# Storing the routed rows from two queues, and the order of four other steps between a router and its expert loop

## The reference

```
v_in = rms_norm(h, norm_ffn_w)                       # 512 rows of 1024
g_logits = vf @ w_rg + b_rg                          # 4 groups; the best one is kept
e_sel = e_logits of that group                       # 8 experts; the best two are kept
gate = softmax(top_v) * p_g                          # two gates for each token
# tokens are sorted by expert into padded blocks, one block at least per expert here
hu = v_pad[tok_b] @ w_e_in[e]                        # 1024 -> 2 x 512
y  = (silu(a) * u) @ w_e_out[e] * gate               # 512 -> 1024, added into the token's row
```

## Time and profile before

| | us |
|---|---|
| median of three executions | 2727.82 (2725.10 to 2729.26) |
| the profiled execution | 2725.17 |
| its span in the profile | 2723.9 |
| `Route` and what leads to the first expert product | 706 to 743 |
| the expert loop | 743 to about 1205 |

### The profile page before, as it was taken

One profiled execution on the slowest core, in us unless ns is written; L12 is line 12 of the kernel. 1 busy time (PEld: TensorE's weight loads), 2 busy tenths in 40 slices (PEclk: granted clock), 3 DMA queues, 4 the chain that ended last, 5 costly groups with the idle time before them and its releaser, 6 DMA issues.

```text
span 2723.9 us, 38632 instructions
## 1 busy us (share of the span) xinstructions
PE 2627.2 (96%) x16282; PEld 2065.9 (76%) x16282; DVE 1286.9 (47%) x2277; ACT 898.7 (33%) x1328; POOL 148.7 (5%) x201
## 2 busy tenths in 40 slices
PE   8999999999999989999999999999999999999997
PEld 6778888778744333349999999988879786788885
DVE  4445666534423333356344465544544434644444
ACT  4334555333221111123222243444444322432222
POOL 0000000000100000000000000031230400000000
PEclk9999999999899999999999999999999999999998
DMA  3012212144599999963222222211111222322221
GB/s 144 16 64 66 61 58 62 58 140 139 218 414 420 421 420 421 420 285 117 94 86 94 81 76 83 96 59 51 59 59 44 66 93 87 103 99 93 93 90 57
DMA packets 78203, 381.62 MB, mean 140 GB/s; under 512 B 9944, under 2 KB 10200, under 8 KB 52816
## 3 DMA queue, kind: packets, MB, share of 16 engines
q1 hardware_dynamic: 71856, 357.14, 35.7%
q0 software_dynamic: 5456, 20.11, 1.9%
q10 hardware_dynamic: 720, 1.90, 0.2%
HBM read 372.67 MB, written 10.62 MB: 141 GB/s over the span
## 4 chain that ended last, share of the span: by engine, by line
PE 74%; DMA 8%; DVE 4%; SPq 2%; ACT 2%; issue 1%; DVEq 0%; ACTq 0%
PE ps L208 72%; DMA rmore<-in_w_ein 5%; DMA ring<-in_w_ein 2%; SPq L293 2%; PE ps L212 1%; DVE ringr L581 0%; PE ps L1963 0%; DMA ring<-in_w_hg 0%; ACT L218 0%; ACT ringr L575 0%; DVE hT L2666 0%; DVE uT L472 0%; ACT hdd L1230 0%; DVE hT L3958 0%; DVE mgb L3955 0%
## 5 line engine op out<-in xcount | busy, mean ns | idle before, releaser
L208 PE MATMUL ps<-uh,ringr 128*128 128x264 f32 (+1 forms) x2256 | 553.8, 340 | 4.4 <-DVE uTr L619 2.4
L208 PEld LDWEIGHTS ps<-uh,ringr 128*128 128x128 f32 x2256 | 366.6, 189 | 48.7 <-DVE uTr L619 3.6
L208 PE MATMUL ps<-buh,ringr 128*128 128x512 f32 (+1 forms) x1312 | 347.2, 351 | 4.4 <-ACT hg L1212 3.3
L208 PE MATMUL ps<-uTr,ringr 128*128 128x512 f32 (+1 forms) x1136 | 350.5, 345 | 0.0
L581 DVE TENSOR_TENSOR ringr<-ring,ringr 128x1024 fp32r<-128x1024 f32 (+1 forms) x215 | 258.2, 1212 | 141.2 <-ACT ringr L575 140.6
L575 ACT CAST ringr<-ring 128x1024 fp32r<-128x1024 f32 (+1 forms) x215 | 219.4, 1036 | 92.8 <-DMA ring<-in_w_fi 34.3
L208 PEld LDWEIGHTS ps<-buh,ringr 128*128 128x128 f32 x1312 | 218.9, 189 | 35.5 <-issue 7.4
L208 PEld LDWEIGHTS ps<-uTr,ringr 128*128 128x128 f32 x1136 | 197.4, 189 | 22.5 <-issue 3.1
L208 PE MATMUL ps<-ful,ringr 128*128 128x264 f32 (+1 forms) x648 | 169.9, 323 | 0.2 <-DVE ful L508 0.2
L208 PE MATMUL ps<-fhh,ringr 128*128 128x264 f32 (+1 forms) x576 | 123.7, 321 | 0.0
L2627 DVE TENSOR_TENSOR fsg<-ps,fsg 128x528 f32<-128x528 f32 (+1 forms) x44 | 30.8, 700 | 193.5 <-PE ps L208 189.7
(11 more groups left out here) (485 smaller groups left out, 4553.5 us busy)
## 6 DMA issues: line engine op xcount, KB each, us to landing
rmore<-in_w_ein SPq DMA_DIRECT2D x51, 1024.0 KB, 27.0
eahead<-in_w_ein SPq DMA_DIRECT2D x47, 1024.0 KB, 26.7
ring<-in_w_ein SPq DMA_DIRECT2D x30, 1024.0 KB, 27.0
rmore<-in_w_eout SPq DMA_DIRECT2D x27, 1024.0 KB, 27.0
ring<-in_w_fi SPq DMA_DIRECT2D x54, 512.0 KB, 3.7
ring<-in_w_eout SPq DMA_DIRECT2D x19, 1024.0 KB, 27.3
eahead<-in_w_eout SPq DMA_DIRECT2D x18, 1024.0 KB, 27.3
fmore<-in_w_fi SPq DMA_DIRECT2D x34, 512.0 KB, 3.7
```

What stands on the lines that cost most here:

```text
L208: return self.P.matmul(out, lhsT, rhs, start=start, stop=stop, skip_group_check=True)
```

## The change

Five edits, all in `Route` but the last:

- The stores of rows 1 and 3 are issued by ScalarE, right after it has written the block, from its own DMA queue, instead of by GpSimd. GpSimd keeps rows 0 and 2.
- ScalarE makes the fourth block of rows before the second exponential (`vexp`) instead of behind it. The store of row 3 goes with it.
- VectorE works out the count of blocks between the two groups of pick products, instead of behind the second group, the overflow lists, the gates and a square of the meta tokens (`meta_dve`).
- The semaphores of the two stores come from the set for hardware queues.
- The idle products ahead of expert 0 go from 11 to 6.

```diff
-        self.rows = [sig.pdma(f"rows{i}") for i in range(4)]
+        self.rows = [(sig.dma if i % 2 else sig.pdma)(f"rows{i}") for i in range(4)]
@@ row_act
             A.activation(self.sent[:, i, 512 * j:512 * j + 512], ps[:, b + j, :], ACT.Copy, scale=self.rt[:, i:i + 1]).then_inc(
                 self.rowed.next(), 1)
+        if i % 2:
+            A.wait_ge(*self.rowed.at(2 * i + 2))
+            A.dma_start(self.k.vrow[128 * i:128 * i + 128, :], self.sent[:, i, :]).then_inc(self.rows[i].landing(), 16)
@@ act
         self.row_act(1)
         self.row_act(2)
+        self.row_act(3)
         v2 = self.s[:, 5, 0:4]
         A.wait_ge(*self.vdiff.at(1))
         A.activation(v2, v2, ACT.Exp).then_inc(self.vexp.next(), 1)
-        self.row_act(3)
@@ pool
-        for i in range(4):
+        for i in (0, 2):
             G.wait_ge(*self.rowed.at(2 * i + 2))
@@ place_dve
         V.tensor_scalar(self.pair, k.ps[:, b, 0:NE // 2], -1.0, float(S), MUL, ADD).then_inc(self.given.next(), 1)
-        V.wait_ge(*self.pick.at(2))
-        over = k.ps[0:64, b + 1, NBLK:NBLK + NOV]
-        V.tensor_scalar(self.more, over, -1.0, float(S), MUL, ADD).then_inc(self.given.next(), 1)
-        V.tensor_scalar(self.tokens, over, -1.0, float(S), MUL, ADD).then_inc(self.given.next(), 1)
-        V.tensor_copy(self.gates, k.ps[:, b + 1, 0:NBLK]).then_inc(self.given.next(), 1)
-        self.nxt.meta_dve()
         V.tensor_tensor(self.cmp, end[0:1].unsqueeze(1).to_broadcast([1, NOV, 32]),
                         iota[0:1, 0:NOV].unsqueeze(2).to_broadcast([1, NOV, 32]), ALU.is_le).then_inc(s.next(), 1)
         V.wait_ge(*s.last())
...
         V.tensor_copy(self.ov[:, 0:1], end[0:1, 31:32]).then_inc(self.blocks.next(), 1)
+        V.wait_ge(*self.pick.at(2))
+        over = k.ps[0:64, b + 1, NBLK:NBLK + NOV]
+        V.tensor_scalar(self.more, over, -1.0, float(S), MUL, ADD).then_inc(self.given.next(), 1)
+        V.tensor_scalar(self.tokens, over, -1.0, float(S), MUL, ADD).then_inc(self.given.next(), 1)
+        V.tensor_copy(self.gates, k.ps[:, b + 1, 0:NBLK]).then_inc(self.given.next(), 1)
+        self.nxt.meta_dve()
@@ Experts.pe
-        self.k.busy(6, 11)
+        self.k.busy(6, 6)
```

## The result

The changed kernel takes 2729.36 us (median of 20 executions, 2725.00 to 2732.88). The kernel before, on the same chips, takes 2725.92 (20 executions, 2723.71 to 2729.26). The ratio is 1.0013, 95% interval 1.0008 to 1.0019: **3.4 us slower**. That is inside the stated range and inside the 0.2% that was called no change. But it is clear of noise and of the other sign than the forecast of -0.6 us.

The account below looks back on a forecast made before the run. The loop's end was taken to be set by when the weight stream resumes behind the hole, after expert 0's first slot. Earlier gather -1.2 us plus clock +0.6 gave -0.6 us: 2727.2 us against a median of 2727.82, range 2722.7 to 2731.

Parts of the forecast that it names:

- The hole as the only path: Weight stream ahead of expert loop: the first expert product moves the hole's end and, one for one, the kernel's end.
- Stores: Row stores ahead of the gather: with a second queue, 105 GB/s each, the last lands at about 729.6 instead of 734.4.
- `vexp`: ScalarE's second exponential, behind the fourth block: comes at 720.0 to 720.4 instead of 719.71, a delay taken as 0.4 us.
- GpSimd ... clears `xg` earlier; nobody waited for that: GpSimd loses two store issues of 0.53 us and clears the gather's buffer earlier; no cost was counted.
- The list at 730.75: Index list `idx` that the gather needs: 730.34 before, plus 0.4 us from the delay of `vexp`.
- The gather's 8.4 us: First gather, issued at 731.85, takes 8.4 us and lands at 740.2 against 740.97; first product 1.2 us earlier, at 741.65.
- Case 2: First gather keeps its 5.5 us: product at 738.8, -2.3 to -4.1 us, 2724.6 us; chance 0.15.
- The clock, +0.6 us: Expert 0 starts at the half level in most executions; 1.8 us for one slow slot, 2.8 for two, 0.6 taken on average.
- How the clock got there: TensorE ahead of expert 0: 12 idle products at the half level, 2.7 us, then a pause of about 3 us.
- Case 3: First two slots of expert 0: half clock costs more than the gather gives, +1.6 to +2.8 us, 2729.4 us; chance 0.17.
- Cases 4 and 5: Row 3's store served late, past 734.4, +4.9 us, chance 0.08; second queue brings nothing, 0 within 0.5 us, chance 0.10.
- "Same" at 0.92: Whole kernel: chance 0.92 of no change beyond about 0.2%, 5.5 us; faster 0.05, slower 0.03.

Follow-up runs that it names:

- the early clearing: Kernel before the change, with GpSimd's clearing of `xg` moved ahead of its store of row 3; ratio 1.0002 (0.9993 to 1.0011).
- the decisive run: Changed kernel with 24 idle products ahead of expert 0 instead of 6, nothing else; ratio 1.0000 (0.9992 to 1.0009) to the kernel before.
- the clearing later: Changed kernel with GpSimd clearing `xg` only when VectorE has the sum of both choices; ratio 1.0007 (0.9999 to 1.0016) to the kernel before.
- all five loads held: Changed kernel with SP's last five loads ahead of the loop waiting for the first gather's landing; ratio 1.0013 (1.0004 to 1.0022) to the kernel before.
- three loads and 6 idle products: Changed kernel, clearing late, 6 idle products, SP's last three loads held until the second pick group ends; ratio 0.9990 (0.9981 to 0.9999) to the kernel before.

## Why the prediction was wrong, step by step

- **The hole as the only path: right in the main.** The stream's lag of 1.20 MB stays constant through the loop, and over the kernels with the full backlog the ratio roughly follows the hole's end. But the prediction gave as a sign of being wrong that the loop's end moves by something that the hole doesn't, and it moved by 4.8 us against 2.7; that part is open.
- **Stores: right in direction and nearly in size.** The last one was expected at 729.6; it was issued at 719.61, took 11.2 us and landed at 730.8, ahead of the list. The rule of the Trainium skill weighed there (page "DMA: Bandwidth & Descriptors", section "Issuing engines are not separate DMA queues"), that issuing from several engines saves only issue time, was not borne out: four stores were there 17.2 us after the first one's issue instead of 20.8. Row 3 was issued 1.75 us earlier here, but with the two stores alone, where it was issued as late as before, they were there after 17.3 us too. The estimate behind 729.6, 105 GB/s for each queue, was not measured by itself.
- **`vexp`: right.** Expected at 720.0 to 720.4, found at 720.01. ScalarE's queue was held for 0.35 us.
- **"GpSimd ... clears `xg` earlier; nobody waited for that": the first step that failed, a term put at nothing.** Nobody waits for its result, but VectorE waits for the clearing itself: 0.69 us on the chain. I had looked at who reads the outcome of a moved instruction, not at what it runs beside.
- **The list at 730.75: missed, 732.54.** 0.3 us are `vexp`, 0.7 the clearing. The rest, 1.2 us, is in idle products: TensorE waited 1.14 us for VectorE, the clock fell within 724 to 725, and the 24 idle products behind took 7.23 us instead of 5.6 and were now what the pick products waited for. I had costed the delay of the chain at its own length and overlooked that a fixed number of idle products takes longer at the half level. This 1.2 us doesn't belong to the change alone: with the fewer idle products or the early clearing, edits that touch nothing of this chain, the list stood at 17.8 too, behind pauses of 1.84 us, since in those executions the idle products behind the rows' transposes began 1.7 us earlier.
- **The gather's 8.4 us: right, and with it that most of the earlier issue is lost.** It took 8.4. A fixed time behind the issue is not what the runs show, though: with the full backlog the gather landed 26.5 to 28.3 us after row 0's store whether it was issued at 18.3 or at 22.0, and issued at 19.9 and 20.0 it landed at 28.3 and 27.5. So what the late list costs by the landing isn't fixed by these single executions. The upper end of the prediction, 741.4, "since the bytes of the stretch are the same", lies nearest: 741.9. Case 2, a quick gather, is out: 7.5 to 8.9 us in every kernel that issued it by 20.0 with the backlog there.
- **The clock, +0.6 us: the term of the sum that failed in size, and the one that the decisive run is about.** The text said that expert 0 would start at the half level "in most executions", priced that at 1.8 us for one slot, and then took 0.6. The profile shows 1.74 us for the first slot and 0.4 for the transposes, which ran at the half level too, 2.1 us in all. With the price of one slot in full, the sum would have been -1.2 + 1.8 = +0.6, slower. The run with 24 idle products gives the 3.4 us back with the list as late as in the changed kernel, while the earlier list alone (the clearing later) gave nothing that is clear of noise.
- **How the clock got there: partly wrong.** The prediction had it low since 730 to 732 and not yet up again. Here it was up: the idle products ran at the full level, the pause was 5.58 us instead of about 3 (half a microsecond from their earlier end, 1.7 from the later landing), and the clock fell at the end of the pause. The pause was seen, but the half level was laid to too short a run of idle products. With all five loads held the run was as short, 12 instructions, the pause 0.59 us, and expert 0 took 7.09 us.
- **The two misses together.** The first product came at 743.82, not at 741.65: 1.8 us for the late list, if it is taken in full, and 0.4 for the slow transposes. So the profile's account is +0.97 + 1.74 = +2.7, beside 3.4 between the medians. Either miss by itself would have turned the sign: -0.6 + 1.8 = +1.2 for the list, +0.6 for the clock.
- **Case 3 is what happened in its mechanism,** given 0.17 and +1.6 to +2.8 us; measured +3.4. Its sum is made of other parts, though: it had the first product 1.2 us earlier and two slow slots at 2.8, and the profile has the product 0.97 later and 1.74 until the first slot is free. Cases 4 and 5 are out: row 3 landed at 730.8.
- **"Same" at 0.92 was right by the bound of 0.2%**, and 2729.36 lies in the range, with some luck: the range was built on a median of three, 2727.82, and that kernel's median of 20 is 2725.92. The same range about that would end at 2729.1. What was wrong is the likeliest value and its sign.

## What to carry to other kernels

Idle products are timed work: when a step is sped up ahead of them, they move with it and end too early, so their number has to be set anew against the landing that they bridge. Before a gather or load on the path is issued earlier, look at what stands in the DMA queues: beside a backlog most of an earlier issue is lost again (issued 3.6 us earlier, landed 0.9 earlier), and here the hole behind the backlog was the place for the last two bulk loads. And when an instruction of GpSimd is moved, look at which small VectorE instructions it now runs beside, not only at who waits for its result.

## What the hardware showed that was not expected

**GpSimd's clearing and VectorE's tensor_scalar.** In the four profiles in which this instruction (four elements for each partition, 0.17 us otherwise) was due during the clearing, it ended 0.03 to 0.04 us after the clearing's end: clearing until 721.08, 722.25, 723.63 and 723.72, the instruction until 721.11, 722.28, 723.66 and 723.76, taking 0.86, 0.43, 0.85 and 0.89 us. In all the others it took 0.17. The Trainium skill has the rule, page "SBUF — State Buffer", section "Who interferes with whom": a tensor_scalar of VectorE can use a port pair that it shares with GpSimd, and the later of the two then waits for the whole of the other. The trace agrees. It agrees too in that VectorE's tensor_tensor and tensor_reduce instructions beside a clearing, in the kernel before, took no longer than elsewhere (0.42 us for 256 elements). Had this page been read next to the moved clearing, the 0.7 us would have been in the sum. That it is the clearing, the run with the clearing moved alone shows; that the cause is the port rests on these four cases and the rule, since the experiment that was to force it missed its moment.

**The clock ahead of expert 0.** Over the 14 profiles of the table, the pauses of TensorE ahead of the transposes were 0, 0, 0, 0, 0.47, 0.49, 0.59 and 0.68 us where the four slots took 7.09 us, and 1.57, 1.75, 2.01, 2.39, 5.58 and 6.68 us where they took 8.63 to 10.08. Ahead of the rank products it was likewise: pauses of 0.17 to 0.67 us in eight profiles, with 5.60 or 5.61 us for the 24 idle products behind, and pauses of 1.14 to 2.11 us in six, with 7.23 or 7.24. A pause of 1.1 to 2.4 us, which I had not counted as a danger, went with a loss of 1.5 to 3 us each time. These are single executions, and the step at which the clock falls differs between them: in the changed kernel just ahead of the transposes, with three loads and 6 idle products within 740 to 741, behind them. That the pause is the cause was tested for the longest alone, by filling it.

**A gather beside a stream.** 512 KB by indices: 3.4 us with the DMA engines free, 3.4, 4.8 and at most 6.4 with three or two of the last loads held back, 7.5 to 8.9 beside the full backlog or the released loads, 5.5 to 5.7 where it was issued so late that the stream was ending.
